# Prompt logits of two key heads as a pair of 64-row products in the attention stages of a streaming encoder

## The reference, cut to what matters

```python
s_idx = jnp.einsum('qhd,sd->qhs', qib, kis).astype(jnp.float32) * IDX_DIM ** -0.5
score = jnp.einsum('qh,qhs->qs', wib.astype(jnp.float32), jax.nn.relu(s_idx))
...
logits = jnp.einsum('qgrd,qkgd->qgrk', qg, kg).astype(jnp.float32) * HEAD_DIM ** -0.5
...
logits = jnp.where(ok[:, None, None, :], logits, NEG_INF)
p = jax.nn.softmax(logits, axis=-1).astype(vg.dtype)
return jnp.einsum('qgrk,qkgd->qgrd', p, vg).reshape(nq, N_HEADS * HEAD_DIM)
```

## Time and profile before

| | |
|---|---|
| median of 3 runs | 1774.59 us |
| profiled execution | 1774.61 us, span 1772.8 us |
| PE, PEld | 1758.3 us (99%), 1722.3 us (97%), 9914 records each |
| DVE | 1075.5 us (61%) |
| ACT | 707.1 us (40%) |
| POOL | 295.1 us (17%) |
| L967, the prompt logits | 128 records, first 79.3 us, last 1440.7 us |
| granted TensorE clock | full in all 40 slices |

### The profile page before, as it was taken

The page is one execution under the profiler, slowest core; times in us unless marked ns, Lnnn a source line. Parts: engine busy times, 40 slices in busy tenths (PEclk is TensorE's granted clock), DMA queues, the critical chain, the costliest instruction groups (busy, mean ns, idle before and its releaser), DMA issues.

```text
span 1772.8 us, 28029 instructions
## 1 busy us (share of the span) xinstructions
PE 1758.3 (99%) x9914; PEld 1722.3 (97%) x9914; DVE 1075.5 (61%) x1906; ACT 707.1 (40%) x1131; POOL 295.1 (17%) x420
## 2 busy tenths in 40 slices
PE   9999999999999999999999999999999999999998
PEld 8989999999999999999999999999999889999998
DVE  7897755544588755554476665554447877555533
ACT  5365433333377433333222333333323564333331
POOL 5253200001216400001100210000131444000011
PEclk9999999999999999999999999999999999999999
DMA  8312333333333433334334333333355113433441
GB/s 296 112 60 73 118 118 118 118 131 131 119 119 97 143 121 121 123 113 140 131 119 130 113 127 118 118 118 128 124 158 199 62 61 107 136 125 118 130 142 60
DMA packets 63846, 216.97 MB, mean 122 GB/s; under 512 B 7153, under 2 KB 8769, under 8 KB 63521
## 3 DMA queue, kind: packets, MB, share of 16 engines
q1 hardware_dynamic: 59520, 202.25, 34.8%
q0 software_dynamic: 3280, 12.12, 2.3%
q10 hardware_dynamic: 976, 1.70, 0.3%
HBM read 212.38 MB, written 3.66 MB: 122 GB/s over the span
## 4 chain that ended last, share of the span: by engine, by line
PE 95%; DVE 2%; issue 1%; ACT 1%; DMA 0%; POOL 0%; DVEq 0%; ACTq 0%; POOLq 0%
PE bank L789 29%; PE bank L788 28%; PE bank L787 28%; PE bank L967 1%; PE bank L948 1%; PE bank L950 1%; PE bank L949 1%; PE bank L1012 1%; PE bank L991 1%; DVE w_lo L1406 1%; PE bank L973 0%; PE bank L890 0%; PE bank L1018 0%; DMA x<-in_x_t 0%; PE bank L1026 0%
## 5 line engine op out<-in xcount | busy, mean ns | idle before, releaser
L1406 DVE TENSOR_TENSOR w_lo<-raw,w_hi 128x1024 fp32r<-128x1024 f32 x382 | 490.3, 1288 | 306.9 <-ACT w_hi L1126 305.3
L787 PE MATMUL bank<-a_hi,w_hi 128*128 128x400 f32 (+2 forms) x1936 | 673.3, 348 | 1.1 <-DVE w_lo L1406 1.1
L788 PE MATMUL bank<-a_lo,w_hi 128*128 128x400 f32 (+2 forms) x1936 | 665.8, 344 | 0.0
L789 PE MATMUL bank<-a_hi,w_lo 128*128 128x400 f32 (+2 forms) x1936 | 665.4, 344 | 0.0
L1126 ACT ACTIVATE w_hi<-raw 128x1024 fp32r<-128x1024 f32 x382 | 400.0, 1052 | 345.9 <-PE bank L789 337.9
L787 PEld LDWEIGHTS bank<-a_hi,w_hi 128*128 128x128 f32 (+1 forms) x1936 | 362.5, 187 | 5.3 <-issue 1.2
L789 PEld LDWEIGHTS bank<-a_hi,w_lo 128*128 128x128 f32 (+1 forms) x1936 | 364.9, 188 | 0.7
L788 PEld LDWEIGHTS bank<-a_lo,w_hi 128*128 128x128 f32 (+1 forms) x1936 | 362.7, 187 | 2.6
L789 PE MATMUL bank<-h_hi,w_lo 128*128 128x400 f32 (+1 forms) x704 | 240.8, 342 | 0.0
L788 PE MATMUL bank<-h_lo,w_hi 128*128 128x400 f32 (+1 forms) x704 | 240.1, 341 | 0.0
L787 PE MATMUL bank<-h_hi,w_hi 128*128 128x400 f32 (+1 forms) x704 | 239.2, 340 | 0.0
(11 more groups left out here) (262 smaller groups left out, 1795.3 us busy)
## 6 DMA issues: line engine op xcount, KB each, us to landing
raw<-in_w_all SPq DMA_DIRECT2D x382, 512.0 KB, 3.4
bias_p<-rel_scratch POOLq DMA_DIRECT2D x2, 2176.0 KB, 11.2
k_s<-in_ck_t POOLq DMA_DIRECT2D x4, 512.0 KB, 8.3
v_c<-in_cv POOLq DMA_DIRECT2D x2, 1024.0 KB, 15.2
ki_s<-in_cki_t POOLq DMA_DIRECT2D x4, 256.0 KB, 5.3
x<-in_x_t SPq DMA_DIRECT2D x2, 400.0 KB, 6.4
x<-in_x_t ACTq DMA_DIRECT2D x2, 400.0 KB, 6.9
out_v_t<-v_f POOLq DMA_DIRECT2D x2, 400.0 KB, 4.7
```

Of the source, the lines that this page charges most:

```text
L787: pe.matmul(out, wh, hi[:, kc, c0:T], start=(first and n == 0), stop=False)
L788: pe.matmul(out, wh, lo[:, kc, c0:T], start=False, stop=False)
L789: mm = pe.matmul(out, wl, hi[:, kc, c0:T], start=False, stop=(last and n == len(blocks) - 1))
L1406: nc.vector.tensor_tensor(w_lo[:, s, :], raw[:, s, :], w_hi[:, s, :].bitcast(F32), ALU.subtract).then_inc(lo_ready, 1)
```

## The change

Prompt items are computed in pairs. `logits(n)` of an item with gi = 0 calls `prompt_pair(n)`, which waits for the bank of n and the bank of n + 1 and then issues both products: partitions 0 to 63 of `q_t` against partitions 0 to 63 of `kz[:, 0, ...]` into the first bank, then partitions 64 to 127 of `q_t` against the same partitions of `kz[:, 1, ...]` into the second. Each contracts 64 rows, so the zeros are no longer read. `logits(n + 1)` does nothing. The waits are those of the items: for item n + 1 it is `lg_ready` at IB[a] + n, which means that item n - 1 is reduced. Sample and meta items, and everything on the other engines, stay.

```diff
+                def free_logits(n):
                     if n < 2:
                         pe.wait_ge(evacuated, t0 + 12 + n)
                     else:
                         pe.wait_ge(lg_ready, IB[a] + n - 1)
-                    ps = logit_bank(a, n)[:, 0:keys]
+                    return logit_bank(a, n)
+
+                def prompt_pair(n):
+                    _, gp, (t, gi, r) = ITEMS[a][n]
+                    keys = width(ITEMS[a][n])
+                    pe.wait_ge(evacuated, t0 + 9 + 4 * gp + r + 1)
+                    both = [free_logits(n), free_logits(n + 1)]
+                    for half in range(2):
+                        rows = slice(64 * half, 64 * half + 64)
+                        pe.matmul(both[half][:, 0:keys], q_t[rows, 4 * gp + r, 128 * t:128 * t + 128], kz[rows, half, gp, 0:keys],
+                                  start=True, stop=True).then_inc(lg_done, 1)
+
+                def logits(n):
+                    kind, gp, what = ITEMS[a][n]
+                    keys = width(ITEMS[a][n])
                     if kind == "prompt":
-                        t, gi, r = what
-                        pe.wait_ge(evacuated, t0 + 9 + 4 * gp + r + 1)
-                        mm = pe.matmul(ps, q_t[:, 4 * gp + r, 128 * t:128 * t + 128], kz[:, gi, gp, 0:keys], start=True, stop=True)
-                    elif kind == "sample":
+                        if what[1] == 0:
+                            prompt_pair(n)
+                        return
+                    ps = free_logits(n)[:, 0:keys]
+                    if kind == "sample":
```

More of the change, by code:

```diff
@@ L954, in dense @@
                         mm.then_inc(half_done, 1)
-                def logits(n):
-                    kind, gp, what = ITEMS[a][n]
-                    keys = width(ITEMS[a][n])
+                def free_logits(n):
                     if n < 2:
```

## The result

The changed kernel takes 1783.03 us, the median of six runs (1782.84 to 1784.75), against 1774.58 for the kernel before in six; the ratio is 1.0049, with a 95% interval of 1.0039 to 1.0059. That is +8.4 us, slower; the prediction said 1782.4. The profiled execution has a span of 1781.0 us, 8.2 over the span before.

What follows compares the result with a forecast made beforehand. TensorE, with 95% of the chain, was taken as the bound, VectorE being full too in the first halves. Terms 5.6 + 1.0 + 1.2 = +7.8 us on 1774.6 gave 1782.4 us; the range leaving out 2 in 10 was 1773 to 1791.

Steps and rivals of the forecast that it cites:

- TensorE's price of a pair: Attention pairs: 0.65 us for 144 keys (now 0.50), 0.86 for 272 (now 0.92); +1.4 us on TensorE alone.
- First halves: First eight pairs of layers 0 and 3: the double wait makes TensorE 2.8 us late in each, +5.6 us.
- the lag of 1.20 at n = 14: First half of layer 0: product 14 starts 1.20 us before reduction 13 ends; a pair must wait for that end.
- Standing still: First half of layer 0, n = 4 to 12: VectorE idles until the pair's first result comes, 1.1 us in all.
- The opening: Start of the first half: pair 0 waits for both banks, pair 2 comes late; VectorE loses 0.3 and 0.3 us.
- Second halves: Second eight pairs of each layer: a few late waits cost +1.0 us in layer 0 and +1.2 in layer 3.
- the wait at n = 33: Second half of layer 0: the pair waits for reduction 32 and dense products begin behind it, +0.7 us with drift.
- VectorE's wait for the pair: Sign in the trace after: VectorE's wait for the new product line grows by 2 to 4 us.
- Waits of TensorE for `nmx`: Sign in the trace after: waits at six pairs or more of each first half, several us against 4.9 now.
- B: Rival for the pairs: the array halves don't run together, passes go one by one; 1790 us, chance 0.12.
- D: Rival for the pairs: shape switches cost little and the halves overlap; about 1768 us, chance 0.13.
- C: Rival for the double wait: VectorE makes up for it, only TensorE's own +1.4 is left; 1776 us, chance 0.17.

Runs made afterwards that it cites:

- e3: The changed kernel with both products of a pair on partitions 0 to 63, the second with wrong queries and keys: 1789.01 us.
- e2: The kernel before with products on 64 rows, each at its own step with its own wait: 1790.98 us.
- e8: The changed kernel with the second bank's wait behind the first product instead of ahead of it: 1779.75 us.
- e6: The changed kernel without VectorE's searches for the largest sample scores in steps 4 to 12 of both core stages: 1779.75 us.
- e9: The changed kernel with items 0 and 1 of each layer computed as before, at their own steps: 1781.30 us.
- e4: Pairs of 64-row products for gp = 1 alone, with the product of the kernel before for gp = 0: 1777.08 us.
- e1: The changed kernel's order and double wait, but each product contracts all 128 rows as before: 1783.76 us.
- e5: The kernel before without VectorE's searches for the largest sample scores in steps 4 to 12 of both core stages: 1773.76 us.

## Why the prediction came out as it did

The sum was +7.8 us and +8.4 was measured. The mechanism is the one that was forecast; that the number is so close is in part luck, since some terms were off in opposite ways. By its terms:

- **TensorE's price of a pair**, 0.65 and 0.86: measured so, to the 10 ns of the chain. That halves of the array run side by side in this shape too, and that each way costs 0.20, were carried over from column halves and from one 64-row product, and both held (e3, e2).
- **First halves, 2.8 us a layer**: 3.2 in layer 0 and 2.9 in layer 3. In the trace of layer 0 the lag of 1.20 at n = 14 is there, VectorE is 1.8 late at that place (its reduction of item 13 ends at 100.65 for 98.82), 2.0 within the stage, where I had 1.7, and 0.15 pass from the end of the reduction to the start of the pair, for which I had nothing. e8 shows VectorE's share apart from the lag, e6 that it hangs on VectorE's load.
- **Standing still**: from the end of a reduction to the next one's start I took 0.55 and 0.76 us; 0.66 and 0.87 were measured. The 0.11 more are the 0.14 from the end of VectorE's read to the start of the pair, less 0.03 by which the pair's first result comes sooner than the 0.55 I took. The sum over the pairs 4 to 12 was undersized by it, 1.1 for 1.5. VectorE got 0.4 back between them, which I had not counted either: the two errors cancel, and that is luck.
- **The opening**, 0.3 and 0.3 of VectorE a layer: by e9 it is 0.85 with the pair's own price of 0.15. It was undersized by 0.1.
- **Second halves, 1.0 and 1.2**: e4 puts both at 2.5 for 2.2. In the trace of the changed kernel, the last reads of the accumulator in a layer are 3.5 late in layer 0 and 8.3 at the end of layer 3, which makes +0.5 and +1.8. The sum was nearly right and the split between the layers was not: two errors cancel here too. In layer 0 the wait at n = 33 cost 0.3 and not 0.7: TensorE is 3.15 late ahead of it (the transposes at 129.38 for 126.23) and 3.45 behind it (the dense products at 133.50 for 130.05), since the reduction of item 32 is only 2.7 late there. What layer 3 has over its 1.2 was not taken apart.
- **Of what the trace after should show**, VectorE's wait for the pair was said to grow by 2 to 4 us and grew by 7.1 (4.6 to 11.7). I had counted only what lengthens the stages: 3.8 of the growth lie in the first halves, and 3.2 in the second ones, where VectorE waits for TensorE at little cost. Waits of TensorE for `nmx` were said to show at six pairs or more of each first half; they show at five, and pair 14 starts 0.15 behind the read it needs without a gap in TensorE's busy time.

Of the rivals, B (no overlap) is excluded by the pair's 0.66 for 272 keys and by e3; D (cheap switches) by the 0.38 behind each pair and by e2; C (VectorE gives its lateness up) by the table of the stage and by e1. C had the strongest case, and e6 shows what it would have needed: a VectorE with time to spare, and even then part of the loss stays.

What stays open: of the 6.0 us between e5 and e6, 3.7 lie in the first halves by the reductions of item 23, and how they divide between the opening and the pair (4, 5) is not shown; no run takes the search of step 2 away.

## What to carry to other kernels

When two products that alternate between two banks are joined to one step, the second product's wait moves ahead of the first. If the engine that empties the banks is the slower one there, the two engines then take turns; a look at "start of product n against end of reduction n-1" in the trace before shows how much lead there is to lose, and putting the second wait behind the first product got back 3.3 us of 8.4 here. A product on half of the array's rows needs a partner to overlap: between full-shape products it pays 0.40 us (whether neighbours of its own shape would save this no run here shows), and a pair of 272 columns in fp32 just earns that back (0.86 for 0.92 here), one of 144 does not (0.65 for 0.50).

## What the runs showed of the hardware

Two fp32 products on row halves with 128 columns of weights each run in the time of one (0.66 with the way in, against 1.11 for two on one half, e3). The Trainium skill, "TensorE: Matmul & The Clock Gate", Part 3, says that weight loads overlap matmuls in flight only where the row groups differ. The trace of the kernel before does not bear out the "only". Its dense products all use the full shape, each with a load of its own:

```profile
79.49 0.44 PE L948 MATMUL bank<-a_hi,w_hi 128*128 128x400 f32 x1
79.59 0.19 PEld L949 LDWEIGHTS bank<-a_lo,w_hi 128*128 128x128 f32 x1
...
79.77 0.35 PE L949 MATMUL bank<-a_lo,w_hi 128*128 128x400 f32 x1
```

The load takes 0.19 us and starts 0.10 after the product ahead of it, and in the chain a load and its product take 0.18 together, so the loads run beside products on the same rows. The way in and the way out cost about the same 0.20 us for one product (e2) and for two, and the way in costs nothing more where TensorE stands waiting anyway: from a standstill L970 reaches VectorE after 0.52 us with 144 keys, and the full-shape pair of e1 after 0.52 as well.
